# Two readerless products and three modulation blocks in other places of TensorE's list in the mixer of a two-layer diffusion step

## What is computed

```
mod = silu(c) @ ada_w[l] + ada_b[l]        # 1024 -> 6 x 1024: shift, scale, gate, twice; one row for
                                           # context tokens, one for latent tokens
h   = rmsnorm(x) * (1 + scale1) + shift1
P   = h @ w_in                             # columns for four mixers
      A: differential attention, 4 heads   B: HGRN2 gated linear recurrence, 4 heads, forward and backward
      C: neighbourhood attention, 4 heads  D: real part of a 2-D DFT
x   = x + gate1 * concat(A, B, C, D) @ w_out
h2  = rmsnorm(x) * (1 + scale2) + shift2
x   = x + gate2 * MoE(h2)                  # 16 experts, top-1 group, then top-2
```

## Time and profile before

| | |
|---|---|
| median of 3 runs | 1229.93 us (1221.55 to 1231.03) |
| the profiled execution | 1229.87 us |
| its span, first to last instruction | 1228.2 us |
| mean granted TensorE clock | 0.945 |
| TensorE matmuls busy | 1109.6 us, 90% of the span |
| VectorE / ScalarE / GpSimd busy | 558.6 / 355.9 / 234.7 us |
| moved by DMA | 325.09 MB, mean 265 GB/s |
| mod_rows (L1844), 384 passes | 58.3 us |

### The profile page before, as it was taken

How to read it: one execution, slowest core, us unless ns; L and a number is a source line. 1 busy time by engine, 2 the same in 40 slices (tenths; PEclk the granted TensorE clock), 3 DMA queues, 4 the chain that set the end, 5 groups by cost and what they waited for, 6 DMA issues and landing times.

```text
span 1228.2 us, 18292 instructions
## 1 busy us (share of the span) xinstructions
PE 1109.6 (90%) x6948; PEld 520.5 (42%) x6948; DVE 558.6 (45%) x1342; ACT 355.9 (29%) x661; POOL 234.7 (19%) x339
## 2 busy tenths in 40 slices
PE   3999999899999987898899999998997999888886
PEld 1545556454443332333244655554544333232332
DVE  1275666743463332323265747666155433223327
ACT  2223445532323221221131424453223322221212
POOL 1222273411010111101020324541200011011100
PEclk9999889889989999999899998997998999899998
DMA  9939731656499999999790412046716799999995
GB/s 364 317 137 170 127 115 58 229 206 274 176 361 379 396 390 407 398 401 401 313 361 18 146 69 83 21 175 250 291 69 249 270 391 397 396 403 407 395 388 189
DMA packets 51214, 325.09 MB, mean 265 GB/s; under 512 B 6710, under 2 KB 7126, under 8 KB 32576
## 3 DMA queue, kind: packets, MB, share of 16 engines
q1 hardware_dynamic: 39296, 293.16, 61.1%
q0 software_dynamic: 10560, 26.17, 8.5%
q10 hardware_dynamic: 1280, 4.72, 0.9%
HBM read 316.15 MB, written 22.25 MB: 276 GB/s over the span
## 4 chain that ended last, share of the span: by engine, by line
PE 60%; DMA 22%; DVE 12%; issue 3%; ACT 2%; SPq 1%; DVEq 0%; ACTq 0%; POOLq 0%
PE ps L2216 19%; DMA ring<-moe_w_up 18%; PE ps L1828 14%; PE ps L1903 7%; PE ps L2106 7%; PE ps L1844 3%; DMA ring<-ada_w 3%; DVE attT L1318 2%; PE ps L1867 2%; PE ps L2000 2%; PE ps L2029 2%; DVE dbuf L1294 1%; PE ps L2205 1%; PE ps L1862 1%; DVE small L1427 1%
## 5 line engine op out<-in xcount | busy, mean ns | idle before, releaser
L2216 PE MATMUL ps<-ring,dbuf 128*32 128x512 f32 x2432 | 421.9, 605 | 35.0 <-DMA ring<-moe_w_up 23.5
L2216 PE MATMUL ps<-extra,dbuf 128*32 128x512 f32 x1312 | 248.9, 624 | 14.3 <-DMA ring<-moe_w_up 13.5
L2216 PEld LDWEIGHTS ps<-ring,dbuf 128*32 128x32 f32 x2432 | 115.3, 111 | 231.2 <-issue 220.6
L1828 PE MATMUL ps<-ring,extra 128*128 128x512 f32 (+1 forms) x384 | 150.6, 552 | 0.0
L1604 DVE COPY dbuf<-ps 128x256 f32<-128x256 f32 (+1 forms) x32 | 15.4, 483 | 212.3 <-PE ps L2205 212.3
L1903 PE MATMUL ps<-extra,ring 128*128 128x384 f32 x320 | 110.1, 503 | 0.0
L2216 PEld LDWEIGHTS ps<-extra,dbuf 128*32 128x32 f32 x1312 | 68.7, 114 | 89.5 <-issue 76.3
L866 POOL DMA_INDIRECT expert_rows<-big,lst x28 | 26.3, 940 | 409.6 <-DVE big L1626 205.2
L1828 PEld LDWEIGHTS ps<-ring,extra 128*128 128x128 f32 x384 | 74.3, 195 | 70.2 <-issue 66.7
L2106 PE MATMUL ps<-ring,extra 128*128 128x512 f32 x192 | 84.3, 594 | 3.0 <-DVE extra L1493 1.8
L1903 PEld LDWEIGHTS ps<-extra,ring 128*128 128x128 f32 x320 | 62.2, 197 | 42.7 <-issue 4.9
(11 more groups left out here) (310 smaller groups left out, 1452.9 us busy)
## 6 DMA issues: line engine op xcount, KB each, us to landing
extra<-moe_w_gate SPq DMA_DIRECT2D x32, 2048.0 KB, 17.3
ring<-moe_w_up SPq DMA_DIRECT2D x32, 2048.0 KB, 23.3
ring<-moe_w_down SPq DMA_DIRECT2D x30, 2048.0 KB, 22.3
ring<-ada_w SPq DMA_DIRECT2D x24, 2048.0 KB, 8.7
ring<-w_in SPq DMA_DIRECT2D x12, 2048.0 KB, 19.9
ring<-w_out SPq DMA_DIRECT2D x4, 2048.0 KB, 7.8
extra<-moe_w_down SPq DMA_DIRECT2D x2, 2048.0 KB, 15.9
skew_rows<-rpb_pad POOLq DMA_DIRECT2D x1, 3810.0 KB, 66.9
```

What stands on the lines that cost most here:

```text
L1828: ins = pe.matmul(out, a, b, start=(n == 0), stop=(n == len(pairs) - 1))
L2216: return pe.matmul(p[QT * g:QT * (g + 1), :], a, w, start=start, stop=stop, tile_position=(0, QT * g))
```

## The change

In DENSE, block 0 moves from (4, 0) to (1, 3); the others follow, so that (4, 0) and (4, 1) keep a block (now 1 and 2), the one of (4, 2) goes to (4, 3), the one of (5, 0) is gone, (5, 1) keeps block 4, (5, 2) has block 5 behind the turn of the first group, (5, 3) has block 6, and behind the loop only block 7 is left. In `decayed_keys`, ahead of unit 1's wait for s_X in each layer, TensorE claims the bank of the transposes that follow and runs two products into it that the transposes overwrite.

```
-         (4, 0): [("ada", 0)], (4, 1): [("ada", 1)], (4, 2): [("ada", 2)], (5, 0): [("ada", 3)], (5, 1): [("ada", 4)],
-         (5, 2): [("mod", 4)], (5, 3): [("ada", 5), ("bo", 1), ("bo", 2)]}
+         (1, 3): [("ada", 0)], (4, 0): [("ada", 1)], (4, 1): [("ada", 2)], (4, 3): [("ada", 3)], (5, 1): [("ada", 4)],
+         (5, 2): [("mod", 4), ("ada", 5)], (5, 3): [("ada", 6), ("bo", 1), ("bo", 2)]}
...
                 def decayed_keys(u):

                     dirs = (0, 1) if UNITS[u][0] == 0 else (UNITS[u][0] - 1,)
+                    if u == 1:
+                        begin(pe, ("kd", l, u))
+                        keep_running(2, bank(("kd", l, u))[0])
                     pe.wait_ge(s_X, l * NUNIT + u + 1)
...
                 gate_spread(l, 0)
-                for n in (6, 7):
-                    dense(("ada", n))
+                dense(("ada", 7))
```

## The result

| | before | after |
|---|---|---|
| median | 1230.4 us (1221.55 to 1234.07, 19 runs) | 1222.94 us (1216.97 to 1225.62, 19 runs) |
| ratio to before, 95% interval | | 0.994 [0.9924, 0.9956] |
| span of the profiled execution | 1228.2 us | 1219.7 us |
| mean granted TensorE clock | 0.945 | 0.958 |

The change makes the kernel faster by 0.6%, 7.5 us. The forecast was 1204, with 1196 to 1219 as its range: 19 us too low, and the range does not reach the result either. By the bound of 1% it is "within 1%", which had 0.13.

A forecast was written before the change was run, and what follows sets the result against it. TensorE was taken as 60% of the span, with 71.1 us of the mixers at half clock behind short waits. Terms 6.8 + 7.8 + 3.0 + 8.6 = 26.2 off 1229.9 gave 1204, range 1196 to 1219.

The forecast's parts named there:

- Term 1: Unit 1: two products fill the wait ahead of the keys and the clock stays at 1.00; 6.8 us gained.
- Term 2: Unit 2: block 0 ahead of the keys hides the wait and ends the low clock behind it; 7.8 us gained.
- Term 3: Unit 4 into unit 5: block moved to unit 4's step 3, taken at low clock; 1.5 us a layer, 3.0 gained.
- Term 4: Unit 5 and behind: no wait at step 3, blocks at full clock, one block in the tail; 8.6 us gained.
- What passes through: Expert phase to the end: its weight issues move earlier too, so all of the mixers' gain reaches the end.
- (a): Clock held in only one early place, or half the gain given back in the expert phase: 1216 us, chance 0.15.
- (b): Clock falls where it fell despite the fillers, only idle time is filled: 1226 us, chance 0.09.

The follow-up runs named there:

- blocks_shifted: The changed kernel with block 2 moved from (4, 1) to (4, 2) and block 4 from (5, 1) to (5, 0): 1207.61 us.
- before_add8: The kernel before with only GpSimd's bias addition cut into eight pieces: 1228.23 us, ratio 1.0015.
- shifted_add8: The changed kernel with GpSimd's bias addition in eight pieces and blocks 2 and 4 moved to (4, 2) and (5, 0): 1199.8 us.
- after_again: The changed kernel run once more, unchanged, for a second profile: 1222.13 us.
- no_products: The changed kernel without the two readerless products ahead of unit 1's keys, blocks left where the change put them: 1227.36 us.
- before_again: The kernel before run once more, unchanged, for a second profile: 1229.86 us.
- products_only: The kernel before with only the two readerless products added ahead of unit 1's keys: 1223.01 us.
- tail_filled: shifted_add8 with block 7 moved behind the transposes of the mixers' outputs, ahead of w_out: 1200.81 us.

## Why the prediction was wrong

**Term 1 (6.8): right, 6.3.** 3.0 and 3.3 us in unit 1, and the clock at 1.00.

**Term 2 (7.8): right in its stretch, 7.5, and lost behind it.** The block costs 0.7, with 0.8 worked out, and from the keys to the values it is 4.2 and 4.6 us less. The step that failed is the one left out. The forecast says that VectorE "moves with" TensorE, and follows VectorE no further than the s_X of unit 2. It never asks for GpSimd, whose one long piece near unit 2 does not move with unit 2's values but with unit 1's exponents. The profile of before had it: the addition at 180.91 and VectorE's L1429 at 186.04 were 0.6 us apart, end to start, and the forecast was about to bring the second forward by nearly 4 us more than the first (3.5 came). The runs with the addition in pieces show this to be the whole of the 8.8 us.

**Term 3 (3.0): wrong sign, +2.6.** The first half holds: the wait 2.31, the block at 3.53. The step that failed is "Step 0 of unit 5 then lasts 5.7 us as before". It had run at half clock before; now the clock was back at 241, step 0 took 3.0 us (from the keys at 240.77 to the values at 243.76), and with the scores of step 1 TensorE was done at 245.0, and so came to VectorE's reciprocal 1.49 us too soon. The forecast had this as its upper bound, since "VectorE was without a gap before it"; that is a reason why nothing can be gained there, and behind this wait the clock fell again, so the low stretch that was one became two. The run with shifted blocks shows that it was the placing: between the same marks it takes 3.2 and 3.9 us less, with three blocks there instead of two.

**Term 4 (8.6): right, 8.4.** The blocks take 1.92, and there is no wait at unit 5's step 3.

**What passes through: not all.** The units of both layers are 12.3 us shorter, the span 8.5, the median 7.5. The rest of the span is 948.6 and 948.7 us in the two executions of before, 952.4 and 953.0 in the two of after. But over all kernels it lies between 948.3 and 954.0 with no order by the gain: blocks_shifted has 949.2 with units 22.8 us shorter, before_add8 has 952.3 with the loop as before. The waits for expert weights do not explain it: they are 39.3 and 42.1 us in the two executions of after, but also 37.1 and 39.9 in the two of before, whose rest is the same within 0.1. What makes the 4 us was not found; it stays open.

**The rivals.** The result lies between (a), 1216, and (b), 1226, but by the mechanism of neither: the clock was held at both early places. The gain was lost at a third place, through a wait that no rival named. The argument against (b), that the rows show 1.00 everywhere TensorE's list is full, misreads: from 144.6 to 151.4 it is full and has 0.50. (a) has the right thought, that half is given back, and looks for it in the expert phase. Over the executions on one chip the granted clock is 0.950 in the mean for before (17) and 0.969 for shifted_add8 (6), a factor of 1.020, and their medians are 29.3 us or 2.4% apart, with filled waits in it too. The rule of the Trainium skill, in "TensorE: Matmul & The Clock Gate", Part 1, that a model of the time needs under 1% for the ramp, does not hold for this kernel by these figures, and by half of the 71.1 us of the earlier trace rows.

## What to carry to other kernels

A stretch that is made earlier arrives at everything behind it, so for each step that comes forward by d, list what each of the other engines does within d ahead of it, and ask of each piece whether it moves by the same d; here it was the long piece of an engine off the critical path that didn't. A long instruction on GpSimd is a candidate for cutting into pieces where VectorE's small operations meet it in a chain that TensorE waits for, even if the pieces take longer in all; where they don't meet, it brought nothing here. Work used to fill a wait belongs directly ahead of the wait, one block for one wait, and the stretch must be read again with the clock at full speed, where the next engine's pace is the new bound.

## What the runs showed of the hardware

- A VectorE multiplication on 128x2 numbers (L1429), 0.17 us by itself, lasts until the end of a GpSimd addition of 128x2048 (4.5 us) within which it starts. That happened ten times in the profiles, and each time the two ended within 0.1 us of each other: 2.89 and 2.91 us in after, 2.53 and 2.97 in after_again, 2.85 and 2.92 in no_products, 3.53 and 2.85 in blocks_shifted, and, started late in the addition, 1.31 in before_again and 0.95 in products_only. With the addition in pieces of 0.72 to 0.95 us it was 0.72 or less. The maxima (L1427, two in 1.02 us) right before it ran at their usual length inside the same addition. The Trainium skill, "SBUF — State Buffer", section "Who interferes with whom", says this of tensor_scalar and tensor_reduce: the first can use the port pair that VectorE shares with GpSimd, which is locked for a whole instruction by whoever came first, the second never does. The traces agree with it in each of these rows. They do not test the second half by itself, since the maxima read PSUM here and the multiplication reads SBUF.
- With TensorE full from 166 to 181 at 1.00, the wait of 2.38 us left a mean clock of 0.57 from 182 to 190; the one of 1.49 us left 0.53 from 247 to 254. In the same step of the same layer, block 3 behind a wait of 0.30 and one of 0.59 ran at 3.57 us in shifted_add8 and at 1.92 in tail_filled. The wait of 2.27 us ahead of unit 1's keys was followed by half clock in nine layers of ten, and by 1.00 in layer 0 of before_add8. The price of a short wait is thus some 3 to 4 us more than itself (half of 6 to 8 us), or nothing.
- In layer 0 the sixteen bias transfers also wait for the transfer into skew_rows. Where that has landed, they start behind GpSimd's exponents (after 166.38, shifted_add8 166.25); where it has not, GpSimd waits for it (4.74 us in after_again, start 170.22; 9.16 in tail_filled, start 175.20). The addition comes 11.6 to 11.8 us behind their start; so whether the collision hurts in layer 0 differs from one execution to the next.
